# Gated units of a six-layer network: one 512-column product for both operand parts, summed at eviction

## The reference, cut to what matters

```python
def swiglu(h, w_gu, w_down):
    g, u = jnp.split(h @ w_gu, 2, axis=-1)
    return (jax.nn.silu(g) * u) @ w_down

# in the four layers of the first block
x = x + swiglu(rms_norm(x, norm_ffn[i]), ffn_w_gu[i], ffn_w_down[i])
# in the second block, for x and ctx, before and after the mixer
x = x + 0.5 * mx[2] * swiglu_2(modulated_norm(x, norm_g[l, 0], mx[0], mx[1]), *ffn1)
```

## Time and profile before

| what | us |
|---|---|
| median of 3 runs | 3873.91 |
| lowest and highest run | 3860.84, 3877.05 |
| span of the profiled execution (first to last instruction) | 3866.5 |
| TensorE busy in it | 3718.8 |
| GpSimd, ScalarE, VectorE busy | 2635.9, 1881.5, 1620.5 |
| mean granted clock of TensorE, 1 = 2.4 GHz | 0.987 |

### The profile page before, as it was taken

One profiled execution on the slowest core, in us unless ns is written; L12 is line 12 of the kernel. 1 busy time (PEld: TensorE's weight loads), 2 busy tenths in 40 slices (PEclk: granted clock), 3 DMA queues, 4 the chain that ended last, 5 costly groups with the idle time before them and its releaser, 6 DMA issues.

```text
span 3866.5 us, 93381 instructions
## 1 busy us (share of the span) xinstructions
PE 3718.8 (96%) x36101; PEld 3538.4 (92%) x36101; DVE 1620.5 (42%) x3499; ACT 1881.5 (49%) x2746; POOL 2635.9 (68%) x1186
## 2 busy tenths in 40 slices
PE   8998998999899898899999999999999999999998
PEld 7778997998699767799999999999999999999998
DVE  6544315315642664433222474753223222276442
ACT  5325446544454431545555555465555555555643
POOL 5005873885288400388888878768888888886886
PEclk9999999999999999999999999999999999999999
DMA  6555662664366355466666646546666666664664
GB/s 187 197 194 145 190 175 80 185 194 121 84 188 191 109 184 190 122 190 190 191 191 194 192 143 190 154 144 203 193 191 191 190 185 199 188 188 130 184 180 141
DMA packets 1162954, 664.98 MB, mean 172 GB/s; under 512 B 30157, under 2 KB 1122201, under 8 KB 1162551
## 3 DMA queue, kind: packets, MB, share of 16 engines
q1 hardware_dynamic: 1162679, 661.06, 57.9%
HBM read 659.92 MB, written 1.05 MB: 171 GB/s over the span
## 4 chain that ended last, share of the span: by engine, by line
PE 57%; issue 26%; POOL 12%; DVE 3%; ACT 1%; DMA 1%; POOLq 0%; DVEq 0%; SPq 0%; ACTq 0%
PE bank L861 55%; POOL wlo L621 12%; PE bank L840 1%; DVE bank L3060 1%; DMA raw<-in_w_in 0%; PE bank L1062 0%; ACT whi L631 0%; DMA raw<-in_ffn_w_gu 0%; PE bank L961 0%; POOLq L620 0%; DVE W L1985 0%; DVE W L1998 0%; DVE W L1983 0%; POOLq L101 0%; PE bank L2701 0%
## 5 line engine op out<-in xcount | busy, mean ns | idle before, releaser
L621 POOL TENSOR_TENSOR wlo<-raw,whi 128x1024 fp32r<-128x1024 f32 (+3 forms) x1182 | 2635.7, 2247 | 1206.8 <-ACT whi L631 1200.6
L631 ACT ACTIVATE whi<-raw 128x1024 fp32r<-128x1024 f32 (+3 forms) x1182 | 1171.5, 996 | 1066.5 <-PE bank L861 905.0
L861 PE MATMUL bank<-AH,whi 128*128 128x256 f32 (+1 forms) x5712 | 1595.6, 279 | 24.2 <-DVE AL L771 9.8
L861 PE MATMUL bank<-AL,whi 128*128 128x256 f32 x5712 | 1588.1, 278 | 0.0
L861 PE MATMUL bank<-AH,wlo 128*128 128x256 f32 (+1 forms) x5712 | 1587.5, 278 | 0.0
L861 PEld LDWEIGHTS bank<-AH,whi 128*128 128x128 f32 x5712 | 1079.0, 189 | 33.5 <-issue 19.4
L861 PEld LDWEIGHTS bank<-AH,wlo 128*128 128x128 f32 x5712 | 1077.7, 189 | 0.0
L861 PEld LDWEIGHTS bank<-AL,whi 128*128 128x128 f32 x5712 | 1076.9, 189 | 0.6
L861 PE MATMUL bank<-HH,whi 128*128 128x256 f32 x1936 | 538.1, 278 | 0.0
L861 PE MATMUL bank<-HH,wlo 128*128 128x256 f32 x1936 | 536.0, 277 | 0.0
L861 PE MATMUL bank<-HL,whi 128*128 128x256 f32 x1936 | 536.0, 277 | 0.0
(11 more groups left out here) (449 smaller groups left out, 4911.7 us busy)
## 6 DMA issues: line engine op xcount, KB each, us to landing
raw<-in_ffn_w SPq DMA_DIRECT2D x420, 512.0 KB, 4.0
raw<-in_w_in SPq DMA_DIRECT2D x182, 512.0 KB, 3.9
raw<-in_ffn_w_gu SPq DMA_DIRECT2D x176, 512.0 KB, 3.8
ada_raw<-in_w_ada SPq DMA_DIRECT2D x96, 512.0 KB, 5.8
raw<-in_ffn_w_down SPq DMA_DIRECT2D x64, 512.0 KB, 3.8
raw<-in_rw_w_rkv SPq DMA_DIRECT2D x48, 512.0 KB, 3.7
raw<-in_w_ada SPq DMA_DIRECT2D x48, 512.0 KB, 5.8
raw<-in_ffn_w SPq DMA_DIRECT2D x56, 384.0 KB, 3.5
```

The lines of the kernel that those rows point to most:

```text
L621: pool.tensor_tensor(wlo[slot][:, 0:n], raw[slot][:, 0:n], whi[slot][:, 0:n], ALU.subtract).then_inc(lo_ready, 1)
L631: act.activation(whi[slot][:, 0:n], raw[slot][:, 0:n], ACT.Copy).then_inc(hi_ready, 1)
L861: mm = pe.matmul(ps[:, 0:o.shape[2]], w, o[:, k0 + c, :], start=tile not in started and c == n == 0, stop=last_panel and c == nk - 1 and n ...
```

## The change

In the `.up` of every gated unit but f21x, and in the `.down` of all eleven, the three matmuls of a block become two. The low and high operand parts now lie so that one instruction reads both: for `.up` the chunk's low part (256 columns) directly ahead of its high part in one buffer `AHL`, for `.down` in the two halves of `HHL`, two runs of 256 columns. The high weights meet both parts in one matmul of 512 columns that writes the whole bank, one half for each part; the low weights meet the high part in one of 256 columns that adds to the first half. VectorE sums the two halves:
- `.up`, explicit units: `dve_sum` (a `tensor_reduce` over pairs that lie 256 columns apart) of the gate bank to bank 6, where silu now reads it, and of the up bank to bank 5; then product, rounding and rest as before. ScalarE does the silu after the up panel's `act_round` instead of ahead of the gate panel's.
- `.up`, ffn0 to ffn3: the same two sums, each followed by the multiplication with `RSTD` in place.
- `.down`: two residual instructions per tile, one for each half, the second waiting for the first.

f21x's `.up` keeps its three matmuls and its eviction. The buffers' total size is the same. The diff, without the passing of the flag `halves` through `Projection`, `dense` and `pair`, without renamings that change no work, and without the counts of the loops:

```diff
@@ -247,7 +249,7 @@
         SLOT = KPAN * P
-        AW = S + 64
+        AW = 2 * S + 64
         raw = [sb(f"raw{i}", SLOT) for i in range(RING)]
@@ -256,7 +258,7 @@
         a_at = place[0]
-        AH, AL = sb("AH", C * AW, F32R), sb("AL", C * S, F32R)
+        AHL = sb("AHL", C * AW, F32R)
         VEC = sb("VEC", C * AW, at=a_at)
@@ -274,8 +276,8 @@
             W.append(sb(f"W{i}", C * S))
-        HH = sb("HH", FC * S, F32R, at=w_at[0])
-        HL = sb("HL", FC * S, F32R, at=w_at[0] + FC * S * 4)
+        HHL = sb("HHL", 2 * FC * S, F32R, at=w_at[0])
+        HH, HL = HHL[:, 0:FC * S], HHL[:, FC * S:2 * FC * S]
         OUTH = sb("OUTH", C * S, F32R, at=w_at[7])
@@ -439,11 +441,12 @@
-        AH_v, AL_v = v3(AH, AW), v3(AL)
+        AH_v, AL_v = v3(AHL, AW)[:, :, S:AW], v3(AHL, AW)[:, :, 0:S]
         A = (AH_v[:, :, 0:S], AL_v)
+        A_BOTH = (AH_v[:, :, 0:S], AL_v, v3(AHL, AW)[:, :, 0:2 * S].rearrange("p c (k t) -> p c k t", k=2))
         A_SHIFTED = (AH_v[:, :, 0:S + 2], AL_v)
         OUT = (v3(OUTH), v3(OUTL))
-        HID = (v3(HH), v3(HL))
+        HID = (v3(HH), v3(HL), HHL[:, :].rearrange("p (k c t) -> p c k t", k=2, t=S))
         BR = (v3(BRH), v3(BRL))
@@ -457,9 +460,9 @@
-        def plan_ffn(name, w_gate, gate_col, w_up, up_col, w_down, operand=A):
-            plan(pair(f"{name}.up", w_gate, gate_col, C, w_up, up_col, C, F, operand, operand))
-            plan(dense(f"{name}.down", w_down, 0, D, HID, kc=FC))
+        def plan_ffn(name, w_gate, gate_col, w_up, up_col, w_down, operand=A_BOTH):
+            plan(pair(f"{name}.up", w_gate, gate_col, C, w_up, up_col, C, F, operand, operand, halves=len(operand) == 3))
+            plan(dense(f"{name}.down", w_down, 0, D, HID, kc=FC, halves=True))
@@ -792,9 +795,9 @@
             if not split_for and not any(host == name for host, _ in FILL_AT):
-                dve_tiles(dve, name, take_residual(dve, x, gate))
+                dve_tiles(dve, name, take_residual(dve, x, gate, g.halves), {dve_step: 1} if g.halves else None)
                 return
-            tile = dve_tiles(dve, name, take_residual(dve, x, gate), by_hand=True)
+            tile = dve_tiles(dve, name, take_residual(dve, x, gate, g.halves), by_hand=True)
             for s in range(g.steps):
@@ -845,7 +848,8 @@
                 started = set()
-                for k, (_, _, k0, nk, tile, (oh, ol)) in enumerate(g.panels):
+                for k, (_, _, k0, nk, tile, parts) in enumerate(g.panels):
+                    oh, ol = parts[0:2]
                     slot = (g.p0 + j * g.pps + k) % RING
@@ -857,6 +861,11 @@
                         wh, wl = (t[slot][:, c * P:(c + 1) * P] for t in (whi, wlo))
+                        if g.halves:
+                            pe.matmul(ps[:, :].rearrange("p (k t) -> p k t", k=2), wh, parts[2][:, k0 + c],
+                                      start=tile not in started and c == 0, stop=False)
+                            mm = pe.matmul(ps[:, 0:S], wl, oh[:, k0 + c, :], start=False, stop=last_panel and c == nk - 1)
+                            continue
                         for n, (w, o) in enumerate(((wh, oh), (wh, ol), (wl, oh))):
@@ -918,11 +927,20 @@
-        def take_residual(dve, x, gate=None):
+        def take_residual(dve, x, gate=None, halves=False):
...
                 o = x[:, bass.ds(s * S, S)]
-                if gate is None:
+                if halves and gate is None:
+                    dve.tensor_tensor(o, o, banks[0][:, 0:S], ALU.add).then_inc(dve_step, 1)
+                    dve.wait_ge(dve_step, after(dve, dve_step))
+                    dve.tensor_tensor(o, o, banks[0][:, S:2 * S], ALU.add).then_inc(bank_free, 1)
+                elif halves:
+                    k = gate[:, bass.ds(s, 1)]
+                    dve.scalar_tensor_tensor(o, banks[0][:, 0:S], k, o, ALU.mult, ALU.add).then_inc(dve_step, 1)
+                    dve.wait_ge(dve_step, after(dve, dve_step))
+                    dve.scalar_tensor_tensor(o, banks[0][:, S:2 * S], k, o, ALU.mult, ALU.add).then_inc(bank_free, 1)
+                elif gate is None:
                     dve.tensor_tensor(o, o, banks[0][:, 0:S], ALU.add).then_inc(bank_free, 1)
@@ -1025,17 +1043,15 @@
                 g = G[f"{name}.up"]
-                done = sum(x.steps for x in order[:order.index(g)] if x.name.endswith(".up"))
...
-                    if k == 0:
-                        act.wait_ge(hidden_ready, after(act, hidden_ready))
-                        act.activation(silu[j % 2][:, :], bank[(g.t0 + j * g.tiles) % RING][:, 0:S],
+                    if k == 1:
+                        act.wait_ge(gate_ready, after(act, gate_ready))
+                        act.activation(silu[j % 2][:, :], bank[6][:, (j % 2) * S:(j % 2 + 1) * S],
                                        ACT.Silu).then_inc(silu_ready, 1)
-                silu_of.per = {hidden_ready: 2}
-                counts.start(act, hidden_ready, done - 2)
-                act_panels(act, g.name, silu_of)
+                silu_of.per = {gate_ready: 2}
+                act_panels(act, g.name, then=silu_of)
                 return
@@ -1070,21 +1086,34 @@
+        def dve_sum(dve, dst, ps):
...
+            return dve.tensor_reduce(dst.unsqueeze(2), ps[:, :].rearrange("p (k t) -> p t k", k=2), AX_X, ALU.add)
...
         def dve_ffn_explicit(dve, name):
-            hidden = bank[5][:, 0:S]
...
-            def take(s, j, banks):
...
+            hidden, up = bank[5][:, 0:S], bank[5][:, S:2 * S]
+            g = G[f"{name}.up"]
...
+            def step(s, j):
...
+                banks = [bank[(g.t0 + j * g.tiles + t) % RING] for t in range(g.tiles)]
+                b = j % 2
+                dve.wait_ge(panels_done, after(dve, panels_done))
+                dve_sum(dve, bank[6][:, b * S:(b + 1) * S], banks[0]).then_inc(gate_ready, 1)
+                dve.wait_ge(panels_done, after(dve, panels_done))
+                dve_sum(dve, up, banks[1]).then_inc(bank_free, 2)
+                dve.wait_ge(bank_free, after(dve, bank_free, 2))
                 dve.wait_ge(silu_ready, after(dve, silu_ready))
                 o = bass.ds(s * S, S)
-                dve.tensor_tensor(hidden, silu[j % 2][:, :], banks[1][:, 0:S], ALU.mult).then_inc(bank_free, 2)
-                dve.wait_ge(bank_free, after(dve, bank_free, 2))
+                dve.tensor_tensor(hidden, up, silu[b][:, :], ALU.mult).then_inc(dve_step, 1)
+                dve.wait_ge(dve_step, after(dve, dve_step))
                 dve.tensor_copy(HH[:, o], hidden).then_inc(dve_step, 1)
...
                 dve.wait_ge(hidden_ready, after(dve, hidden_ready))
-            counts.start(dve, bank_free, G[f"{name}.up"].t0)
-            dve_tiles(dve, f"{name}.up", take, {silu_ready: 1, bank_free: 2, dve_step: 1, hidden_ready: 1})
+            counts.start(dve, bank_free, g.t0)
+            steps_of(dve, g, {panels_done: 4, gate_ready: 0, silu_ready: 2, bank_free: 4, dve_step: 4, hidden_ready: 2}, step)
+            dve.wait_ge(bank_free, tiles_of(f"{name}.up"))
@@ -1107,12 +1136,22 @@
                     dve.tensor_reduce(offset[:, b:b + 1], banks[0][:, S:S + 2], AX_X, ALU.add)
-                dve.tensor_tensor(bank[6][:, b * S:(b + 1) * S], banks[0][:, 0:S], RSTD[:, :], ALU.mult).then_inc(gate_ready, 1)
+                g_in = bank[6][:, b * S:(b + 1) * S]
+                if g.halves:
+                    dve_sum(dve, g_in, banks[0]).then_inc(dve_step, 1)
+                    dve.wait_ge(dve_step, after(dve, dve_step))
+                dve.tensor_tensor(g_in, g_in if g.halves else banks[0][:, 0:S], RSTD[:, :], ALU.mult).then_inc(gate_ready, 1)
                 dve.wait_ge(panels_done, after(dve, panels_done))
...
                     dve.tensor_reduce(offset[:, 2:3], banks[1][:, S:S + 2], AX_X, ALU.add)
-                dve.tensor_tensor(up, banks[1][:, 0:S], RSTD[:, :], ALU.mult).then_inc(bank_free, 2)
-                dve.wait_ge(bank_free, after(dve, bank_free, 2))
+                if g.halves:
+                    dve_sum(dve, up, banks[1]).then_inc(bank_free, 2)
+                    dve.wait_ge(bank_free, after(dve, bank_free, 2))
+                    dve.tensor_tensor(up, up, RSTD[:, :], ALU.mult).then_inc(dve_step, 1)
+                    dve.wait_ge(dve_step, after(dve, dve_step))
+                else:
+                    dve.tensor_tensor(up, banks[1][:, 0:S], RSTD[:, :], ALU.mult).then_inc(bank_free, 2)
+                    dve.wait_ge(bank_free, after(dve, bank_free, 2))
                 dve.wait_ge(silu_ready, after(dve, silu_ready))
```

More of the change, by code:

```diff
@@ L112, with __init__ @@
 class Projection:
-    def __init__(self, name, steps, panels, tokens_out=False, direct=False, by_chunk=False):
+    def __init__(self, name, steps, panels, tokens_out=False, direct=False, by_chunk=False, halves=False):
         self.name, self.steps, self.panels = name, steps, panels
@@ L1128, in dve_ffn @@
             counts.start(dve, bank_free, g.t0)
[L1129 removed]
```

(2 more changed lines are left out.)

19 lines of the change are left out of this document (10 added, 9 removed).

## The result

The changed kernel takes 3922.8 us (median of 4 runs, 3918.7 to 3928.6); beside it the kernel before took 3875.1 (4 runs, 3860.8 to 3877.1). The ratio is 1.0118, 95% interval 1.0091 to 1.0145: slower by more than the 0.5% that can be told, where 3814.8 us and a gain of 1.5% were predicted. The profiled execution has a span of 3920.9 us against 3866.5.

What follows compares the result with a forecast made beforehand. The prediction took the number and distance of TensorE's matmuls to bound the gated units. Its terms, -60.6 - 3.3 + 2.3 + 2.5 = -59.1 us, took the median from 3873.9 to 3814.8 us, range 3798 to 3852.

Steps and rivals of the forecast that it cites:

- The matmuls: Blocks of `.up` and `.down` in gated units: each falls from 340.1 to 329.0 ns, 5456 blocks, 60.6 us gained.
- rows 5 and 6: Earlier profile: float32 matmuls with weight loads 215.6 ns apart; 256-column matmuls at 1.2 GHz starting 0.21 to 0.22 us apart.
- the surplus: Each 256-column matmul in gated units: 6.7 ns of its 113.4 ns distance beyond the 106.7 ns of streaming at 2.4 GHz.
- The 117.8 ns stretch: ffn3's 366 blocks, surplus 11.1 ns a matmul: if only the short ones keep it, 8.9 ns more a block, 3.3 us gained.
- VectorE: Two added sums per `.up` step, 686 ns each: 4.56 us a step in ffn0 to ffn3 against TensorE's 5.26, no cost.
- rival E: VectorE's sums over two half banks cost 1.753 us each, so VectorE binds in `.up`: slower, 3979 us; chance 0.05.
- The tails: `.down` of ffn0, ffn1, ffn2 and f21x: the eighth tile's second residual instruction and hand-off delay the next stage, 2.3 us lost.
- the panel pipeline: `.down` of seven hosts: TensorE waits for GpSimd's weight panels after its 5.0 us pause, 7 x 0.36 = 2.5 us lost.
- C's neighbour: Case that the chip handles 512 columns as two times 256, so the change doesn't do what it says: 3879 us; no chance given.
- B: Rival for gated units' matmuls: the 6.7 ns are paid once per matmul whatever its length, 3842 us; chance 0.18.
- F: Rival: with a load already waiting, the short matmul too goes at 109 ns, 24 us more gained, 3791 us; chance 0.05.
- My upper bound for the 512: The 512-column matmul takes at most two 256-column distances, 226.7 ns, which would give no gain.

## Why the prediction was wrong

**The step that failed** is in "The matmuls": "I take 215.6 ns for the 512 columns, because the two cases nearest in stream time (rows 5 and 6) both lie at 213 to 216, and 113.4 for the 256 that follow". Measured are 235.0 and 118.3: 19.4 and 4.9 ns too little, 24.3 a block, 5456 x 24.3 = 133 us in all. The block of 353.3 ns is beyond the 336 that the prediction itself named as its sign of being wrong. The expected -60.6 us becomes 5456 x (353.3 - 340.0) = +72.6 where the kernel before is fast, and less by what it had in slow stretches: 60.8 in the two profiles' `.up` and `.down` together.

**Why those rows didn't carry it.** In both the stream is long because a column takes twice as long: two cycles each in the float32 sums, if they are read as the prediction reads them, 1.2 GHz in the stage of the earlier trace rows. Neither shows 512 fp32r columns at 2.4 GHz, which nothing in the kernel before did. The same length of stream is not the same case. And the earlier trace rows don't say what was drawn from them, that a long stream hides the surplus: at clock 0.50 matmuls of 128 columns are 213.3 ns apart too, so there the weight load is as slow as the 256 columns, and no surplus shows either way. The Trainium skill, TensorE: Matmul & The Clock Gate, Back-to-back issue gap, gives N/2.4 + 2.5 for an isolated matmul, 215.8 for 512 and 109.2 for 256. The trace disagrees for this data type in both: 226 to 236, and 113.3 or 117.8. The measurement decides.

**What makes up the distance.** I read the earlier trace rows rightly that a load takes as long as 256 columns: 128 columns, at full clock, still take 111.7 ns, and 704 columns in three matmuls take as long as 768. The same page's section on LDWEIGHTS makes it 106.7 ns for 128 columns, an estimate by its formula. The trace has 111.7 for load and matmul together at full clock, and 213.3 at 0.50. What I concluded from it was wrong: one load less saves nothing when the 512 columns that replace two streams cost 231 to 236 ns, at best 226 behind a fast narrow one, which is 2 x 113.3. And a single matmul of another length turned the fast pace into the slow one in all 20 cases. The change puts one into each block, and there each narrow matmul takes 118 and each wide one 235; that the one follows from the other fits, and isn't shown by a run of its own. Even the best case, 226.7 + 113.3 = 340.0, would only have equalled before's block; it never occurs in a row. Groups of eight, with fewer changes, cost 346.7.

**The 117.8 ns stretch** was expected to gain 3.3 us. ffn3 did not: its `.up` and `.down` took 128.2 and 63.9 us before, 127.9 and 65.0 after. Where before is in its slow pace its block takes 353.3 ns, exactly after's. I took this stretch for a feature of ffn3; it is a draw. The profile that I summed against had nearly all units fast, in other executions other units are slow, 4.7 us for each `.up`, which is a part of before's spread. The rest of the program brings another: it takes 1843.0 to 1860.8 us in the profiles of the kernel before and of its versions with extra matmuls, and the kernels with short pairs still spread from 3853 to 3879. After has one pace.

**VectorE**: right. Sums 699 ns for the 686 taken, hidden in `.up` as the run without them shows. Its busy share in ffn0's `.up` is 79.1 of 127.6 us, 62%, for the 67% predicted over a shorter step. The sums behave by their inputs, and rival E was wrong by 2.5 times in its price. VectorE too had a longer step to hide in than predicted, 5.65 us instead of 5.26.

**The tails and the panel pipeline** were to cost 2.3 and 2.5 us. In five of the seven `.down` that host preparations after takes 63.05 us, which is 176 x 0.3533 = 62.2 and 0.9 beside; before had 1.1 beside where it was fast. So there is no new wait for weights, and GpSimd (83 to 85% busy in `.up`, where over 90% was predicted) isn't near its limit. It had more time than predicted, though: 2.83 us a panel, not 2.63. Whether it would have kept up at the predicted pace no run shows. The tails lie in the stretches of everything else, where the first two profiles of before differ by 4.9 us among themselves; 2.3 can't be read there. That the DMA stays hidden was right.

**The rivals.** C's neighbour, "if the chip handles 512 columns as two times 256", 3879, came nearest and had no chance of its own; but it too lacked the 118 behind the wide one. B and F were gains that didn't happen. No rival ended slower by the matmul itself: the slower side was filled with VectorE. My upper bound for the 512, two narrow distances, was a belief that a wide matmul can't cost more than what it replaces; nothing in the rows gave it.

**What stays open**: why equal matmuls have two paces, why one of another length always ended the fast one and two or four left it behind them, and whether the 20 ns on 512 columns belong to the length, to the four-byte operands or to writing a whole bank. No run separates these. Matmuls that share one weight load weren't tried. So the cause is shown down to the matmul and its distance, and no deeper.

## What to carry to other kernels

Where loading weights takes as long as streaming the columns, a bound of "fewer loads" is worth nothing until one matmul of the new shape, in the data type and at the clock in question, has been seen in a trace: price it by itself first, in one unit. And look at the distance between starts in several executions and stages before a baseline is summed against, since a kernel that is nothing but matmuls can run at two paces without a stall in any view. Keep the lengths in a row equal; if the row has to be broken, try a pair: here two of 128 or of 512 columns between 256-column ones left the fast pace behind them. The whole kernel gained 0.3% in one such version and nothing that can be told in the others.

## What the runs showed of the hardware

- Equal fp32r matmuls of 256 columns with 128x128 weights run 113.3 or 117.8 ns apart at 2.4 GHz, for whole projections, in the same kernel and execution. One matmul of 128 or 512 columns between them always turned 113.3 into 117.8 (20 cases) and mostly 117.8 into 113.3 (17 of 22); two leave 113.3 (41 cases in three kernels, 11 of them coming from 117.8; f21x's `.up` apart), and so did four (10 cases, 2 of them from 117.8). No busy share shows the pace: TensorE is 100% busy at both.
- Matmuls of 512 columns of this type: 226 to 236 ns at 2.4 GHz, 233.3 in a row. Of 128: 111.7 at 2.4 GHz (335.0 a block of three), 213.3 at 1.2 GHz (640.0).
- Wide and narrow by turns: 235.0 + 118.3 = 353.3 ns, where three narrow ones take 340.0 or 353.3.
- With 128 columns in place of 256 the granted clock was 0.50 in most of ffn0 to ffn3 and in f11c's `.up`, and 1.00 in f10c, f10x, f20c and f11x, with TensorE 100% busy in both and the same instructions; the time was 4626.7 us. Each of the five falls came right behind 0.9 to 2.6 us of idle time, and the units that stayed at 1.00 had none over 0.1 us. With 256 columns the same idle stretches brought no fall. No run varies the idle time by itself.
